# Half of the columns of the gathered tokens fetched as rows by indirect DMA, and turned late in a pass

## The chip, the cores and the metric

The kernel runs on one core of one Trainium2 chip. The metric is the device time of one execution in microseconds (us). TensorE is called PE, VectorE DVE, ScalarE ACT, GpSimd POOL and SyncE SP; PEld is PE's weight load, which overlaps its matmuls. SP only issues DMAs here.

## What is computed

One layer of a diffusion trunk runs on 384 tokens (128 context tokens and 256 latent ones) of 1024 columns in float32: a norm, four token mixers side by side, a merge, an output projection, then a mixture of experts, and a last norm. The change touches the experts alone:

```python
def block(args):
    rows, e = args
    xb = x_pad[rows]                                   # the tokens of this block, one per row
    return (jax.nn.silu(xb @ w1[e]) * (xb @ w3[e])) @ w2[e]

out = lax.map(block, (row_token, block_expert))        # every expert's tokens, block by block
return segment_sum(out * row_gate[:, None], row_token)[:T]   # each token's 8 experts added up, times their gates
```

There are 64 experts, of which each token takes 8. `w1` and `w3` of an expert are 1024x256, `w2` is 256x1024, so an expert has 3 MB of weights, and all of them are read once or more from memory.

## The kernel before

The token mixers and the router take the first 860 us or so. The routed experts follow, in `experts` (line 2643), in **passes**. A pass handles two **halves** `a_` of 128 places each, and a place is one token for one expert. The places of a half belong to two experts (`u`), in quarters of 32 places: one expert has three quarters and the other one, or each has two. A pass so reads the weights of four experts, 12.6 MB (12 DMAs of 1024 KB).

Everything is done with matrix products on PE:

- `sel` (line 2975, DVE) is a 0/1 matrix, tokens by 256 places, for both halves of the next pass. `gather` (line 2727) multiplies the normed tokens with it, so that `xg` holds the tokens of the 256 places with columns on the partitions, as the products of the experts want them. The tokens stand in two parts, `h2[HI]` and `h2[LO]` (`h_high` and `h_low` in rows), each of three tiles of 128 tokens. So one 128-column block of `xg` takes 6 products of 128x256; a job `G` makes two blocks in one bank, and the four jobs `G` of a pass make all eight.
- `H` (line 2826): the first two weight matrices on `xg`. ACT and DVE make `hid` from it. `HT` (line 2840) turns `hid`.
- `Y` (line 2863): the third matrix, in two jobs of 512 columns. ACT reads each bank into `y[HI]`, and then DVE subtracts that from the bank into `y[LO]` (line 3002), so that a bank of `Y` is free only when both are through.
- `S` (`turn`, line 2746) turns `sel` and the gates for the scatter. ACT reads the gates with four pairs of small instructions (line 2913) and then copies `selT` (line 2917). The copy into `selT` of half 0 also waits for `s_scat`, the end of the scatter that reads the old one.
- `scatter` (line 2735) adds `y` of the other half to the sums of the tokens, in banks 0 to 5, with 12 products in two groups of 6.

**Two banks for all jobs.** Six of PE's eight banks hold the sums. All other products of a pass are **jobs** that take banks 6 and 7 in turn, by their place in the list `JOBS`. `open_bank` lets PE wait until the job two places earlier in the list has been read by its last reader (`readers`: ACT, or DVE after it). ACT and DVE take their jobs in the order of the list too. This list is what sets the order of the work around the change. In the list before, `G` jobs are read by ACT and DVE in turn.

The order on PE in a pass is: half 0: H, scatter (first 6), HT, S of half 1, scatter (last 6), Y, Y; half 1: H, scatter, HT, four G, S of half 0, scatter, Y, Y. A first pass (written out, with the jobs of the router's plan, X and B, in it) and a last one (half 0 alone) stand around a loop. The first gather is made ahead of the first pass by four jobs `G0`.

SP refills the weights: `w13` of a half when its H is done, `w2` when its Y is done (line 3143 and 3147). PE waits for `w2` before the last two blocks of H, and for `w13` of the other half at the end of Y. POOL does nothing in this part until the very end (line 3132).

Of the kernel before, what the change touches and what calls it, by code (L numbers as in the profile page):

```python
# [14 lines left out]
P = 128  # L15
D = 1024
KD = D // P
NT = 3
T = NT * P
# [25 lines left out]
F32 = mybir.dt.float32  # L45
# [149 lines left out]
def trunk(nc, a, o):  # L195

    ctx = ExitStack()
    with ctx:
# [2185 lines left out]
        def _(pool):  # L2384
# [139 lines left out]
            for h in (1, 2, 3):  # L2524
                combine_last("merge", 3, h)
                if h < 3:
                    combine("merge", 3, h + 1)
                add_branch(3, 2 * h, 2 * h + 2)
            expert_work["gpsimd"](pool)


# [72 lines left out]

def expert_tiles(ctx, nc):


    def sb(name, *shape, dt=F32):  # L2610
        return name, ctx.enter_context(nc.sbuf_tensor(name, list(shape), dt))

    return dict([
        sb("xg", P, KD, 2 * P),
        sb("hid", P, FE),
        sb("sil", P, FE),
        sb("hidT", P, 2, P),
        sb("gslot", P, 2),
        sb("gate_parts", P, 2, NT, 2),
        sb("flags", P, 8),  # L2620
        sb("where", P, 16),
        sb("got", P, 4),
        sb("pad", P, 206),
        sb("w13", P, 2, 2, 2, KD, FE),
        sb("w2", P, 2, 2, 2, D),
        sb("sel", P, NT, 8, QUARTER, dt=F32R),
        sb("selT", P, 2, T, dt=F32R),
        sb("y", P, 2, D, dt=F32R),
        sb("quarter_places", P, NT, 8 + NX),
        sb("quarter_gates", P, NT, 8 + NX),  # L2630
        sb("expert_of", P, 2, NX // 4, dt=mybir.dt.int32),
        sb("rounds", P, 2, dt=mybir.dt.int32),
        sb("rowsE", P, 2, T),
        sb("farther", P, T),
        sb("steps", P, 2, 32),
        sb("plan", P, 4, NX),
        sb("turn_by", P, NT, TURN, dt=F32R),
        sb("g2row", P, 2, D),
        sb("final_gain", P, D),
    ])  # L2640


def experts(ctx, nc, a, o, psum, x, h2, mod_parts, ident_r, ident, ss, sq, sums, places, gates, iota, tiles, s_w13, s_rowsT, s_out):


    def sem(name):
        return ctx.enter_context(nc.semaphore(name))
# [10 lines left out]
    gated = spare[:, NT * D:2 * NT * D].rearrange("p (t n) -> p t n", t=NT)  # L2658


    s_filled = sem("job_filled")
    s_read = {"act": sem("act_took"), "dve": sem("dve_took")}
    s_w2 = [sem(f"down_{a_}_landed") for a_ in range(2)]
# [14 lines left out]


    AHEAD = [("G0", 0, j) for j in range(4)] + [("B", 0, 0), ("B", 0, 1), ("X", 0, 0), ("S0", 0, 0)]  # L2680
    GATHERS = [("G", 0, j) for j in range(4)]
    JOBS = [("H", 0, 0), ("HT", 0, 0), ("S", 1, 0), ("Y", 0, 0), ("Y", 0, 1), ("H", 1, 0), ("HT", 1, 0)] + GATHERS + \
           [("S", 0, 0), ("Y", 1, 0), ("Y", 1, 1)]
    JOBS_LAST = [("H", 0, 0), ("HT", 0, 0), ("Y", 0, 0), ("Y", 0, 1)]
    JOBS_FIRST = AHEAD + [("H", 0, 0), ("X", 0, 1)] + JOBS[1:5] + \
                 [("X", 0, 2), ("B", 0, 2), ("X", 0, 3), ("B", 0, 3), ("X", 0, 4)] + JOBS[5:]
# [1 line left out]

    def readers(job):
        kind, _, i = job  # L2690
        return {"H": ("act", "dve"), "HT": ("act",), "S": ("act",), "S0": ("act",), "Y": ("act", "dve"), "X": ("dve",), "B": ("act",),
                "G": (("act",), ("dve",))[i % 2], "G0": (("act",), ("dve",))[i % 2]}[kind]

    READS = {(kind, by): [j for j in LISTS[kind] if by in readers(j)] for kind in LISTS for by in ("act", "dve")}
# [25 lines left out]
    def tensor_part(pe):  # L2720
        mm = nc.tensor.matmul

        def gather(j, out):
            for i in range(2):
                k = 2 * j + i
                for n, (part, t) in enumerate([(part, t) for part in (HI, LO) for t in range(NT)]):
                    last = mm(out[:, i * 256:i * 256 + 256], lhsT=h2[part][:, t, k * P:(k + 1) * P],  # L2727
                              rhs=sel[:, t, :, :], start=n == 0, stop=n == 2 * NT - 1)
            last.then_inc(s_filled, 1)

        def scatter(a_, lo, hi):

# [52 lines left out]
        def body(q, kind, quarters):  # L2785
# [13 lines left out]
            def close_bank(ins):  # L2799
                ins.then_inc(s_filled, 1)  # L2800
# [14 lines left out]
            for a_ in range(1 if last else 2):  # L2815
                H, HT = ("H", a_, 0), ("HT", a_, 0)
                ps = open_bank(H)
                if first and a_ == 0:
                    for by, i in (("act", 2), ("dve", 3)):
                        pe.wait_ge(s_read[by], read(q, by, ("G0", 0, i), kind))  # L2820
                    pe.wait_ge(s_w13[0], 64)
                for k in range(KD):
                    if k == KD - 2:
                        pe.wait_ge(s_w2[a_], 32 * q + 32)
                    for lo, hi, u in quarters:
                        ins = mm(ps[lo:hi, :], lhsT=xg[:, k, a_ * P + lo:a_ * P + hi],  # L2826
                                 rhs=w13[:, a_, u, :, k, :], start=k == 0, stop=k == KD - 1)
                close_bank(ins)

                add = not (first and a_ == 0)  # L2830
                if add:
                    pe.wait_ge(s_read["dve"], read(q, "dve", ("Y", 0, 1), kind) if a_ else read(q - 1, "dve", ("Y", 1, 1)))
                    scatter(1 - a_, 0, 6)
                else:
                    close_bank(plan_step(1, open_bank(("X", 0, 1))))

                ps = open_bank(HT)
                pe.wait_ge(s_read["dve"], read(q, "dve", H, kind))
                for f in range(2):
                    ins = nc.tensor.transpose(ps[:, f * P:(f + 1) * P],  # L2840
                                              hid[:, :].rearrange("s (p f) -> s f p", f=2)[:, f, :], ident[:, :])
                close_bank(ins)

                if a_ == 0 and not last:
                    close_bank(turn(1, open_bank(("S", 1, 0))))
                elif a_:
                    pe.wait_ge(s_sel, q + 2)
                    for job in GATHERS:
                        gather(job[2], open_bank(job))
                    pe.wait_ge(s_gq, q + 2)  # L2850
                    close_bank(turn(0, open_bank(("S", 0, 0))))
                if add:
                    scatter(1 - a_, 6, 12)

                for h in range(2):
                    ps = open_bank(("Y", a_, h))
                    if h == 0:
                        pe.wait_ge(s_read["act"], read(q, "act", HT, kind))
                    for f in range(2):
                        if (h, f) == (1, 1) and not last:  # L2860
                            pe.wait_ge(s_w13[1 - a_], 64 * q + 64 * (1 + a_))
                        for lo, hi, u in quarters:
                            ins = mm(ps[lo:hi, :], lhsT=hidT[:, f, lo:hi], rhs=w2[:, a_, u, f, h * W:(h + 1) * W],  # L2863
                                     start=f == 0, stop=f == 1)
                    close_bank(ins)
                if first and a_ == 0:
                    for i in (2, 3, 4):
                        close_bank(plan_step(i, open_bank(("X", 0, i))))
                        if i < 4:
                            close_bank(gate_row(i, open_bank(("B", 0, i))))  # L2870

        HALVES = [(0, 64, 0), (64, 128, 1)]
        THREE_AND_ONE = [(0, 32, 0), (32, 64, 0), (64, 96, 0), (96, 128, 1)]
# [88 lines left out]
    def vector_part(dve):  # L2962
# [22 lines left out]
        def take(q, job, kind):  # L2985
            what, a_, i = job
            dve.wait_ge(s_filled, filled(q, job, kind))
            if "act" in readers(job):
                dve.wait_ge(s_read["act"], read(q, "act", job, kind))
            ps = bank_of(job, kind)  # L2990
            if what == "H":
                dve.wait_ge(s_gslot, 8 * q + 4 + 4 * a_)
                ins = stt(hid[:, :], ps[:, FE:], gslot[:, a_:a_ + 1], sil[:, :], ALU.mult, ALU.mult)  # L2993
            elif what in ("G", "G0"):
                ins = v.tensor_copy(xg[:, 2 * i:2 * i + 2, :].rearrange("p k n -> p (k n)"), ps)
            elif what == "X" and i < 2:
                ins = v.tensor_copy(got[0:NE, :], ps[0:NE, 0:4])
            elif what == "X":
                ins = table(ps, i - 2)
            else:  # L3000
                hh = slice(i * W, (i + 1) * W)
                ins = tt(y[:, LO, hh], ps, y[:, HI, hh].bitcast(F32), ALU.subtract)  # L3002
            ins.then_inc(s_read["dve"], 1)
# [79 lines left out]
        select_gates(slice(0, 8), 1)  # L3083
        dve.wait_ge(s_copied, 2)
        flag_counts()

        def body(q, kind):
            first, last = kind == "first", kind == "last"
# [39 lines left out]

    def gpsimd_part(pool):
        for t in range(NT):  # L3130
            pool.wait_ge(s_gated, t + 1)
            nc.gpsimd.tensor_tensor(x[:, t, 0:W], x[:, t, 0:W], gated[:, t, 0:W], ALU.add).then_inc(s_added, 1)  # L3132


    def sync_part(sp):
# [17 lines left out]
        for u in range(2):  # L3153
            down(1, u, 2 + u)
        sp.dma_start(fg_row[:, :], a["final_g"].rearrange("(a n) -> a n", a=1).to_broadcast([P, D])).then_inc(s_fg, 16)
        sp.wait_ge(s_read["dve"], read(0, "dve", ("X", 0, 4), "first"))

        def refill(q, a_, at, kind):
# [76 lines left out]
```

## Time and profile before

| | |
|---|---|
| median of 3 runs | 1456.57 us (1455.64 to 1459.07) |
| the profiled execution | 1455.05 us, of which the span from first to last instruction is 1453.2 us |
| granted TensorE clock, mean | 0.992 |
| PE busy | 1414.5 us, 97% of the span |
| DVE, ACT, POOL busy | 554.2, 430.1 and 273.1 us |
| DMA | 310.52 MB |

The profile is that of one execution. A timeline row merges neighbouring instructions of one line; since matmuls overlap one another, the time from one row's start to the next one's start says what a group costs on PE, not its own length. "<-" in a row's idle note names what it waited for. In rows, a product of plain float32 counts as two instructions, one of the rounded type `fp32r` as one; `w` stands for `w13` and `w2`, `arena` and `late` are shared memory, and `late` holds the constants `iota` too.

### The profile page before, as it was taken

How to read it: one execution, taken by the hardware profiler on the slowest of the kernel's cores; microseconds unless marked ns; L12 is line 12 of the kernel's file. 1: busy time of each engine (PE TensorE's matmuls, PEld its weight loads, DVE VectorE, ACT ScalarE, POOL GpSimd, SP SyncE). 2: the span in 40 equal slices, each digit the busy share in tenths (PEclk: the TensorE clock that was granted, in tenths of full speed). 3: DMA queues.
4: the chain of work that ended last, by engine and by line, in shares of the span. 5: the costliest groups of instructions: out<-in, count | busy, mean ns of one | idle time of the engine just before them, and what ended most of it. 6: DMA issues, size and time to landing. Idle time of an engine off the chain costs nothing.

```text
span 1453.2 us, 21489 instructions
## 1 busy us (share of the span) xinstructions
PE 1414.5 (97%) x8214; PEld 1014.5 (70%) x8214; DVE 554.2 (38%) x1116; ACT 430.1 (30%) x1020; POOL 273.1 (19%) x212
## 2 busy tenths in 40 slices
PE   6999999999999989999999999999999999999996
PEld 2795898989988986889987865555455555555552
DVE  3477243875255576434221373111111121111114
ACT  3232221322544362223320322223222232222223
POOL 0440324314054642553141000000000000000001
PEclk9999999999999999999999999999999999999998
DMA  9440422214202439321136343999999999999981
GB/s 377 166 131 27 133 70 105 88 59 145 75 16 85 160 131 361 104 87 59 59 102 196 119 186 151 419 421 402 373 363 378 359 373 378 379 379 378 376 333 44
DMA packets 104386, 310.52 MB, mean 214 GB/s; under 512 B 9216, under 2 KB 69376, under 8 KB 75776
## 3 DMA queue, kind: packets, MB, share of 16 engines
q1 hardware_dynamic: 97984, 306.46, 55.3%
q10 hardware_dynamic: 6336, 3.15, 0.8%
q8 instruction: 45, 0.74, 0.2%
q14 instruction: 21, 0.17, 0.0%
HBM read 306.44 MB, written 3.15 MB: 213 GB/s over the span
## 4 chain that ended last, share of the span: by engine, by line
PE 93%; DVE 2%; DMA 2%; ACT 1%; POOL 0%; issue 0%; SPq 0%; POOLq 0%; DVEq 0%
PE banks L595 20%; PE banks L627 19%; PE banks L2826 16%; PE banks L2863 8%; PE banks L2735 7%; PE banks L2727 7%; PE banks L1016 4%; DMA ring<-in_ada_w 2%; PE banks L602 2%; PE banks L1162 1%; PE banks L853 1%; PE banks L678 1%; PE banks L746 1%; PE banks L1210 1%; PE banks L2746 1%; PE banks L741 1%
## 5 line engine op out<-in xcount | busy, mean ns | idle before, releaser
L2826 PE MATMUL banks<-w,xg 128*64 128x512 f32 (+1 forms) x1312 | 234.0, 595 | 0.0
L2826 PEld LDWEIGHTS banks<-w,xg 128*64 128x64 f32 (+1 forms) x1312 | 73.5, 127 | 154.0 <-issue 134.9
L627 PE MATMUL banks<-hT,ring 128*128 128x192 f32 x792 | 137.8, 327 | 0.8 <-DVE late L1764 0.8
L627 PEld LDWEIGHTS banks<-hT,ring 128*128 128x128 f32 x792 | 129.6, 190 | 3.2 <-DVE late L1764 1.1
L3132 POOL TENSOR_TENSOR x<-x,w 128x512 f32<-128x512 f32 x3 | 4.2, 1429 | 655.7 <-DVE w L3111 655.7
L2863 PE MATMUL banks<-w,hidT 128*64 128x512 f32 (+1 forms) x656 | 120.7, 597 | 0.3 <-ACT hidT L2903 0.3
L2735 PE MATMUL banks<-y,selT 128*128 128x512 f32 x384 | 104.3, 407 | 0.0
L627 PE MATMUL banks<-x,combos 128*128 128x192 f32 x528 | 97.4, 328 | 2.6 <-ACT late L1320 2.6
L627 PE MATMUL banks<-x,ring 128*128 128x192 f32 x528 | 97.0, 327 | 0.9 <-ACT late L1327 0.9
L3002 DVE TENSOR_TENSOR y<-banks,y 128x512 fp32r<-128x512 f32 x66 | 45.6, 691 | 133.1 <-ACT y L2919 133.1
L2735 PEld LDWEIGHTS banks<-y,selT 128*128 128x128 f32 x384 | 67.3, 189 | 37.6 <-issue 26.2
L2993 DVE SCALAR_TENSOR_TENSOR hid<-banks,gslot,sil 128x256 f32<-128x256 f32 x33 | 16.0, 484 | 200.0 <-ACT sil L2901 200.0
L627 PEld LDWEIGHTS banks<-x,combos 128*128 128x128 f32 x528 | 88.1, 191 | 2.8 <-issue 2.8
L627 PEld LDWEIGHTS banks<-x,ring 128*128 128x128 f32 x528 | 86.9, 190 | 1.4 <-ACT late L1327 1.2
L595 PE MATMUL banks<-yT,ring 128*128 128x384 f32 x256 | 85.7, 487 | 0.0
L595 PE MATMUL banks<-ring,hT 128*128 128x256 f32 x384 | 85.5, 385 | 0.0
L2863 PEld LDWEIGHTS banks<-w,hidT 128*64 128x64 f32 (+1 forms) x656 | 34.0, 126 | 69.2 <-issue 68.0
L595 PEld LDWEIGHTS banks<-ring,hT 128*128 128x128 f32 x384 | 73.9, 193 | 10.1
L1016 PEld LDWEIGHTS banks<-arena 128*128 128x128 f32 x568 | 67.6, 192 | 11.5 <-issue 7.8
L2901 ACT ACTIVATE sil<-banks 128x256 f32<-128x256 f32 x33 | 12.7, 383 | 209.2 <-PE banks L2826 209.2
L1016 PE MATMUL banks<-arena 128*128 128x128 f32 x568 | 72.5, 279 | 0.8 <-DVE arena L2284 0.4
L2727 PE MATMUL banks<-sel,h_high 128*128 128x256 f32 x408 | 71.6, 284 | 0.0
(461 smaller groups left out, 2090.2 us busy)
## 6 DMA issues: line engine op xcount, KB each, us to landing
w<-in_exp_w SPq DMA_DIRECT2D x198, 1024.0 KB, 8.9
ring<-in_w_in SPq DMA_DIRECT2D x46, 1024.0 KB, 5.1
ring<-in_ada_w SPq DMA_DIRECT2D x24, 1024.0 KB, 7.8
ring<-in_w_branch SPq DMA_DIRECT2D x8, 1024.0 KB, 6.1
ring<-in_w_out SPq DMA_DIRECT2D x4, 1024.0 KB, 6.5
arena<-in_sh_w SPq DMA_DIRECT2D x3, 1024.0 KB, 7.9
x<-in_x_sample SPq DMA_DIRECT2D x4, 512.0 KB, 8.5
arena<-in_t_last_layer SPq DMA_DIRECT2D x1, 1024.0 KB, 8.3
```

The lines of the kernel that those rows point to most:

```text
L595: last = mm(out, lhsT=lhsT, rhs=rhs, start=i == 0, stop=i == len(pairs) - 1)
L602: last = nc.tensor.transpose(ps[0:n, i * P:(i + 1) * P], src, ident[:, :])
L627: last = mm(out, lhsT=w[:, k, :], rhs=tokens[:, k, :], start=start and k == 0, stop=k == KD // 2 - 1, skip_group_check=not start)
L678: last = mm(ps[g * 32:(g + 1) * 32, :], lhsT=cond[:, k, :], rhs=w[:, g * W:(g + 1) * W], start=k == 0, stop=k == KD - 1)
L741: banks.close(mm(ps, lhsT=fnet[:, (2, 1)[ri], tok[t]], start=True, stop=True, rhs=fw3[:, order * W:(order + 1) * W]))
L1016: last = mm(ps[:, h * P:(h + 1) * P], lhsT=lhsT, rhs=rhs, start=True, stop=True)
L2727: last = mm(out[:, i * 256:i * 256 + 256], lhsT=h2[part][:, t, k * P:(k + 1) * P], rhs=sel[:, t, :, :], start=n == 0, stop=n == 2 * NT - 1)
L2735: ins = mm(psum[:, t * 2 + h, :], lhsT=selT[:, a_, t * P:(t + 1) * P], rhs=y[:, part, h * W:(h + 1) * W], start=False, stop=False)
L2826: ins = mm(ps[lo:hi, :], lhsT=xg[:, k, a_ * P + lo:a_ * P + hi], rhs=w13[:, a_, u, :, k, :], start=k == 0, stop=k == KD - 1)
L2863: ins = mm(ps[lo:hi, :], lhsT=hidT[:, f, lo:hi], rhs=w2[:, a_, u, f, h * W:(h + 1) * W], start=f == 0, stop=f == 1)
L2993: ins = stt(hid[:, :], ps[:, FE:], gslot[:, a_:a_ + 1], sil[:, :], ALU.mult, ALU.mult)
L3002: ins = tt(y[:, LO, hh], ps, y[:, HI, hh].bitcast(F32), ALU.subtract)
```

## The change

Half of the columns (`FROM_ROWS` = 512 of 1024) now come into `xg` another way. Ahead of the loop, POOL adds the two parts of columns 512 to 1023 of all tokens into `whole_rows`, and SP stores these 384 rows of 2 KB in a tensor in memory (`token_rows`). In each pass, PE finds the token number of each place with two new jobs `I` behind the Y jobs of half 0 (3 products with 2 columns each); DVE turns them into integers `row_of_place`; POOL issues two indirect DMAs, one per half, that fetch 128 rows of 2 KB each into `fetched`. Only the first two `G` jobs stay products. The other two, which keep their names in the list, now turn `fetched` with 8 transposes, and stand behind `S` of half 0 and the scatter, just ahead of the Y jobs of half 1.

```diff
@@ gpsimd, end of the mixers' part
+            for t in range(NT):
+                banks.emptied(pool, ("h2", t, 1))
+            pool.wait_ge(s_out.sem, 96)
             expert_work["gpsimd"](pool)
@@ expert_tiles
+        sb("token_ids", P, NT, 2, dt=F32R),
+        sb("row_of_place", P, 2, dt=mybir.dt.int32),
+        sb("fetched", P, 2, D - FROM_ROWS),
+        sb("whole_rows", P, NT, D - FROM_ROWS),
@@ experts
-    GATHERS = [("G", 0, j) for j in range(4)]
-    JOBS = [("H", 0, 0), ("HT", 0, 0), ("S", 1, 0), ("Y", 0, 0), ("Y", 0, 1), ("H", 1, 0), ("HT", 1, 0)] + GATHERS + \
-           [("S", 0, 0), ("Y", 1, 0), ("Y", 1, 1)]
+    GATHERS = [("G", 0, j) for j in range(2)]
+    TURNS = [("G", 0, j) for j in range(2, 4)]
+    JOBS = [("H", 0, 0), ("HT", 0, 0), ("S", 1, 0), ("Y", 0, 0), ("Y", 0, 1), ("I", 0, 0), ("I", 1, 0), ("H", 1, 0),
+            ("HT", 1, 0)] + GATHERS + \
+           [("S", 0, 0)] + TURNS + [("Y", 1, 0), ("Y", 1, 1)]
@@ tensor_part
+        def turn_rows(j, out):
+            for i in range(2):
+                at = (2 * j + i) * P - FROM_ROWS
+                for a_ in range(2):
+                    last = nc.tensor.transpose(out[:, (2 * i + a_) * P:(2 * i + a_ + 1) * P], fetched[:, a_, at:at + P], ident[:, :])
+            last.then_inc(s_filled, 1)
+
+        def rows_of_places(a_, out):
+            for t in range(NT):
+                ins = mm(out[:, 0:2], lhsT=pair_selection(a_, t), rhs=token_ids[:, t, :], start=t == 0, stop=t == NT - 1)
+            return ins
@@ body of a pass on PE, behind the scatter of a half
+                if a_ and not last:
+                    for job in TURNS:
+                        out = open_bank(job)
+                        if job[2] == 2:
+                            pe.wait_ge(s_fetched, 32 * q + 32)
+                        turn_rows(job[2], out)
@@ body of a pass on PE, behind Y of half 0
+                if a_ == 0 and not last:
+                    if first:
+                        pe.wait_ge(s_ids, 1)
+                    pe.wait_ge(s_sel, q + 2)
+                    for i in range(2):
+                        close_bank(rows_of_places(i, open_bank(("I", i, 0))))
@@ vector_part
+            elif what == "I":
+                ins = v.tensor_copy(row_of_place[:, a_:a_ + 1], ps[:, 0:1])
+        for t in range(NT):
+            ins = ts(token_ids[:, t, :], iota[:, 2 * P:2 * P + 1].to_broadcast([P, 2]), float(t * P), None, ALU.add)
+        ins.then_inc(s_ids, 1)
@@ gpsimd_part
+            nc.gpsimd.tensor_tensor(whole_rows[:, t, :], h2[HI][:, t, FROM_ROWS:].bitcast(F32), h2[LO][:, t, FROM_ROWS:].bitcast(F32),
+                                    ALU.add).then_inc(s_whole, 1)
+        pool.wait_ge(s_stored, 16 * NT)
+        def fetch(q, kind):
+            for a_ in range(2):
+                pool.wait_ge(s_read["dve"], read(q, "dve", ("I", a_, 0), kind))
+                ...
+                nc.gpsimd.indirect_dma_start(
+                    fetched[:, a_, :], None, rows[:, :],
+                    bass.IndirectOffsetOnAxis(ap=row_of_place[:, a_:a_ + 1], axis=0)).then_inc(s_fetched, 16)
+        fetch(0, "first")
+        n2 = count(pool, 1)
+        with pool.Fori(1, n2) as q:
+            fetch(q, "mid")
@@ sync_part, behind the load of the last norm's gains
+        for t in range(NT):
+            sp.wait_ge(s_whole, t + 1)
+            sp.dma_start(rows[t * P:(t + 1) * P, :], whole_rows[:, t, :]).then_inc(s_stored, 16)
```

The order of the instructions on PE changes at two places of each pass. The first is the step from Y of half 0 (`w,hidT`) to H of half 1 (`w,xg`), before:

```order
L2863 MATMUL banks<-w,hidT 32x512 [waits act_took]
L2863 MATMUL banks<-w,hidT 32x512 x3
L2861 ISA
L2863 MATMUL banks<-w,hidT 32x512 [waits gate_up_1_landed]
L2863 MATMUL banks<-w,hidT 32x512 x3
L2794 REGISTER_ALU
L2826 MATMUL banks<-w,xg 32x512 [waits dve_took]
```

and now, with the jobs `I` between them (`token_ids,sel`):

```order
L2898 MATMUL banks<-w,hidT 32x512 [waits gate_up_1_landed]
L2898 MATMUL banks<-w,hidT 32x512 x3
L2909 REGISTER_ALU
L2823 REGISTER_ALU [waits selection_ready]
L2757 MATMUL banks<-token_ids,sel 128x2 [waits dve_took]
L2757 MATMUL banks<-token_ids,sel 128x2 x2
L2823 REGISTER_ALU
L2757 MATMUL banks<-token_ids,sel 128x2 [waits dve_took]
L2757 MATMUL banks<-token_ids,sel 128x2 x2
L2823 REGISTER_ALU
L2855 MATMUL banks<-w,xg 32x512 [waits dve_took]
```

H of half 1 followed Y directly; now the six small products stand between, and the second group of three waits for `dve_took` once more than H did: the count stands for the read of the second Y bank there, and for the first one's in the group ahead. The second place is the step from S of half 0 (`turn_by,sel`) over the scatter (`y,selT`) to Y of half 1, before:

```order
L2746 MATMUL banks<-turn_by,sel 128x144 [waits act_took]
L2746 MATMUL banks<-turn_by,sel 128x144 x2
L2735 MATMUL banks<-y,selT 128x512 x6
L2794 REGISTER_ALU
L2863 MATMUL banks<-w,hidT 32x512 [waits act_took,dve_took]
L2863 MATMUL banks<-w,hidT 32x512 x7
L2794 REGISTER_ALU
L2863 MATMUL banks<-w,hidT 32x512 [waits act_took]
```

and now, with the turned rows (`ident,fetched`) between scatter and Y:

```order
L2775 MATMUL banks<-turn_by,sel 128x144 [waits act_took]
L2775 MATMUL banks<-turn_by,sel 128x144 x2
L2764 MATMUL banks<-y,selT 128x512 x6
L2823 REGISTER_ALU
L2752 MATMUL banks<-ident,fetched 128x128 [waits rows_fetched,dve_took]
L2752 MATMUL banks<-ident,fetched 128x128 x3
L2823 REGISTER_ALU
L2752 MATMUL banks<-ident,fetched 128x128 [waits act_took]
L2752 MATMUL banks<-ident,fetched 128x128 x3
L2823 REGISTER_ALU
L2898 MATMUL banks<-w,hidT 32x512 [waits act_took]
L2898 MATMUL banks<-w,hidT 32x512 x7
```

Two groups of four transposes stand there now. The second waits for ACT's read of S, and Y for ACT's read of the first group; before, Y's first job waited for a read of the last gather, which was long past.

## Rows read from the trace of the kernel before

**Rows 1.** Of the page, the busy times; then DMA in 40 slices.

```profile
PE 1414.5 (97%) x8214; PEld 1014.5 (70%) x8214; DVE 554.2 (38%) x1116; ACT 430.1 (30%) x1020; POOL 273.1 (19%) x212
...
DMA  9440422214202439321136343999999999999981
GB/s 377 166 131 27 133 70 105 88 59 145 75 16 85 160 131 361 104 87 59 59 102 196 119 186 151 419 421 402 373 363 378 359 373 378 379 379 378 376 333 44
```

**Rows 2.** The chain of waits in time order, 952 to 986: start us, us, what.

```profile
952.44 6.87 PE banks L2826 x64
...
966.42 6.87 PE banks L2826 x64
...
974.88 0.23 PE banks L2840 x2
975.11 5.61 PE banks L2727 x48
980.72 0.29 PE banks L2746 x3
981.01 1.43 PE banks L2735 x6
982.44 3.57 PE banks L2863 x32
986.01 4.27 PE banks L2826 x37
```

**Rows 3.** All gather products (line 2727): duration ns min/median/max, first and last start.

```profile
L2727 PE MATMUL banks<-sel,h_high x408: 277/280/684, 867.8 to 1417.0; 128*128 128x256 f32 x136
...
L2727 PE MATMUL banks<-sel,h_low x408: 277/278/283, 868.5 to 1417.3; 128*128 128x256 f32 x136
```

**Rows 4.** Timeline by engine around the end of Y of half 0: start us, us.

```profile
966.49 0.60 ACT L2919 ACTIVATE y<-banks 128x512 fp32r<-128x512 f32 x1 [1.12 <-PE banks L2863]
...
965.40 0.69 DVE L3002 TENSOR_TENSOR y<-banks,y 128x512 fp32r<-128x512 f32 x1 [2.55 <-ACT y L2919]
967.12 0.69 DVE L3002 TENSOR_TENSOR y<-banks,y 128x512 fp32r<-128x512 f32 x1 [1.02 <-ACT y L2919]
...
966.14 0.23 PEld L2826 LDWEIGHTS banks<-w,xg 128*32 128x32 f32 x8 [0.63 <-DVE y L3002]
...
966.24 2.75 PE L2826 MATMUL banks<-w,xg 128*32 128x512 f32 x23
```

**Rows 5.** The same around the scatter of half 1.

```profile
979.36 0.60 ACT L2905 ACTIVATE xg<-banks 128x512 f32<-128x512 f32 x1 [2.20 <-PE banks L2727]
...
982.44 0.20 ACT L2913 ACTIVATION_READ_ACCUMULATOR gate_parts<-banks 32x1 f32 x1
982.66 0.49 ACT L2917 ACTIVATE selT<-banks 128x384 fp32r<-128x384 f32 x1
...
982.37 3.64 PE L2863 MATMUL banks<-w,hidT 128*32 128x512 f32 x32
```

**Rows 6.** The first pass, DVE and PE.

```profile
899.96 0.96 DVE L2975 TENSOR_TENSOR sel<-late,quarter_places 128x768 fp32r<-128x768 f32 x1
...
901.04 0.18 DVE L2983 TENSOR_TENSOR turn_by<-quarter_gates,turn_by 128x24 fp32r<-128x24 f32 x1
...
898.90 3.65 PE L2826 MATMUL banks<-w,xg 128*64 128x512 f32 x16
```

**Rows 7.** Two stretches: span, busy by engine, clock, DMA share, GB/s.

```profile
952.16:985.73 33.57, 33.57 (x278) 17.09 (x274) 6.34 (x11) 8.95 (x28) 0.00 (x0) 1.00 1.01 421
...
1120.00:1154.00 34.00, 34.00 (x184) 17.99 (x182) 6.50 (x12) 8.94 (x28) 0.00 (x0) 1.00 0.93 375
```

**Rows 8.** Landing of the weights (line 3143), us from issue.

```profile
DMA to landing us min/median/max: 4.8/9.1/21.7
```

**Rows 9.** Of the page: POOL's addition of 512 columns.

```profile
L3132 POOL TENSOR_TENSOR x<-x,w 128x512 f32<-128x512 f32 x3 | 4.2, 1429 | 655.7 <-DVE w L3111 655.7
```

**Rows 10.** DVE's small read of a bank, ns.

```profile
L2997 DVE COPY got<-banks x2: 144/148/152, 876.2 to 886.7; 64x4 f32<-64x4 f32 x2
```

More of the change, by code:

```diff
@@ L2603, in _ @@
             expert_work["sync"](sp)
+FROM_ROWS = D // 2
 def expert_tiles(ctx, nc):
@@ L2658, in experts @@
     gated = spare[:, NT * D:2 * NT * D].rearrange("p (t n) -> p t n", t=NT)
+    token_ids, row_of_place, fetched, whole_rows = (tiles[n] for n in ("token_ids", "row_of_place", "fetched", "whole_rows"))
+    rows = nc.dram_tensor("token_rows", (T, D - FROM_ROWS), F32, kind="Internal").ap()
+    s_whole, s_stored, s_ids = sem("whole_rows_ready"), sem("token_rows_stored"), sem("token_ids_ready")
+    s_fetched, s_row = sem("rows_fetched"), sem("row_of_place_seen")
     s_filled = sem("job_filled")
@@ L2690, in readers @@
         kind, _, i = job
-        return {"H": ("act", "dve"), "HT": ("act",), "S": ("act",), "S0": ("act",), "Y": ("act", "dve"), "X": ("dve",), "B": ("act",),
+        return {"H": ("act", "dve"), "HT": ("act",), "S": ("act",), "S0": ("act",), "Y": ("act", "dve"), "X": ("dve",), "B": ("act",), "I": ("dve",),
                 "G": (("act",), ("dve",))[i % 2], "G0": (("act",), ("dve",))[i % 2]}[kind]
@@ L3130, in gpsimd_part @@
         for t in range(NT):
+            nc.gpsimd.tensor_tensor(whole_rows[:, t, :], h2[HI][:, t, FROM_ROWS:].bitcast(F32), h2[LO][:, t, FROM_ROWS:].bitcast(F32),
[4 more added lines that the diff above has]
+                pool.wait_ge(s_read["dve"], read(q, "dve", ("I", a_, 0), kind))
+                pool.wait_ge(s_read["dve"], read(q, "dve", ("I", a_, 0), kind))
+                pool.sem_inc(s_row, 1)
+                nc.gpsimd.indirect_dma_start(
[6 more added lines that the diff above has]
+        for t in range(NT):
             pool.wait_ge(s_gated, t + 1)
@@ L3155, in sync_part @@
         sp.dma_start(fg_row[:, :], a["final_g"].rearrange("(a n) -> a n", a=1).to_broadcast([P, D])).then_inc(s_fg, 16)
+        for t in range(NT):
+            sp.wait_ge(s_whole, t + 1)
+            sp.dma_start(rows[t * P:(t + 1) * P, :], whole_rows[:, t, :]).then_inc(s_stored, 16)
         sp.wait_ge(s_read["dve"], read(0, "dve", ("X", 0, 4), "first"))
```

## The prediction

> **What bounds the kernel now.** I read the page's busy times first: PE is busy for 97% of the span, no other engine for more than 38% [rows 1]. In the experts' part the DMA engines are nearly full too (slices 26 on: 9 tenths, 363 to 421 GB/s), so the next question is which of the two sets the pace. The chain of waits says PE: from one H of half 0 (952.44) to the next (986.01) it runs through PE's products alone, and a pass lasts 33.57 us [rows 2]. A pass moves 12.58 MB of weights. In the stretch 952 to 986 the DMA engines catch up on a backlog and reach 421 GB/s, at which those take 29.9 us; later they move only what PE asks for, 375 GB/s at a share of 0.93 [rows 7]. So DMA could follow a pass down to some 30 us, and PE's own sequence is what an edit must shorten. PE's clock is granted in full there (1.00, the 2.4 GHz level), in both stretches.
>
> **What the change removes.** Half the gather products of a pass. The 48 of line 2727 take 5.61 us of the chain [rows 2], 0.117 us each; 24 go, **-2.80 us a pass**. The trace has 816 of them [rows 3], so 17 gathers; one is made ahead and stays, so 16 passes change: the first, and 15 in the loop.
>
> **What it adds at the end of Y of half 0 (jobs I).** Six small products, and a hand-over. Before, H of half 1 took the bank of the first Y job: DVE ends its subtraction at 965.40 + 0.69 = 966.09, PE loads weights at 966.14 and multiplies at 966.24 [rows 4], so 0.15 us from the end of a read to the next product. PE lost next to nothing, because the second Y job ran meanwhile. Now that bank goes to the first job I, and the second I takes the bank of the *second* Y job. ACT reads that one from 966.49 on and DVE is done at 967.12 + 0.69 = 967.81 [rows 4]. PE has nothing to run in between but three small products: the first product of the second I starts at 967.96. Three products with these same `sel` weights and 144 columns take 0.29 us (S [rows 2]); I take that for three with 2 columns as well, since the weight load is the same. H starts at 968.25 instead of 966.24: **+2.01 us**. H also needs DVE's conversion of the first I, 0.15 us [rows 10] from 967.81 on, which with 0.15 us of hand-over allows 968.11, so it does not bind, and that is the lower bound as well: +1.87. The upper: the three at the gather's 0.117 us and one more 0.1 us for a load, +2.2. Nothing is earned back behind H, which PE is then in.
>
> **What it adds between scatter and Y of half 1 (turned rows).** Eight transposes; two of float32 take 0.23 us (974.88 [rows 2]), so four take 0.46. But again the banks decide. The first group takes the bank of the second G, which is long free, and runs at 982.44. The second takes the bank of S, which ACT gives back only after four gate reads (the last ends at 982.44 + 0.20 = 982.64) and the copy of `selT`, 982.66 + 0.49 = 983.15 [rows 5]. ACT then copies the first group into `xg`; the like took 0.60 us (979.36 [rows 5]), so to 983.77. Y's first job takes *that* bank: 983.77 + 0.15 = 983.92, instead of 982.37 [rows 5]: **+1.55 us**. The second group (983.30 to 983.76) fits inside, and DVE's read of it (0.69 us, to about 984.9 with its end and hand-over) is over before Y's second job wants the bank at 983.92 + 1.8. Bounds: the gate reads start 0.3 us behind S whatever else, so little can be gained, +1.4; if ACT's copy starts 0.15 us late, +1.7.
>
> **Sum of a pass in the loop:** -2.80 + 2.01 + 1.55 = **+0.76 us**, with +0.47 to +1.10 as ends. Times 15: +11.4 us.
>
> **The first pass.** There `sel` is made late: DVE ends it at 899.96 + 0.96 = 900.92, while H of half 1 started at 898.90 and the gathers needed `sel` only later [rows 6]. The jobs I need it in front of H: first product at 901.07, three in 0.29 us, the last one's own duration about 0.28 [rows 3] to 901.64; DVE is free from 901.22 [rows 6], converts in 0.15 us, and H starts at about 901.94: +3.0. With -2.80 and +1.55 this is +1.8 us (1.4 to 2.3).
>
> **What I cost at nothing.** POOL's three additions (1.43 us each [rows 9]) and the three stores behind them lie 40 us ahead of the first fetch on engines that wait; even behind weights, whose landings take at most 21.7 us [rows 8], they are in time. If they were not, only the first pass would wait. DVE's three tiny instructions for the token numbers fall into an idle gap, about 0.5 us if not. POOL's own queue holds nothing but fetches until the end. The last pass and the tail are the old ones.
>
> **The fetches** are the unknown: no row shows an indirect DMA. POOL can issue both about 0.4 us behind the start of H (968.6); the first turned row is wanted when the scatter ends, in the new time at 982.44 + 2.01 - 2.80 = 981.65. That leaves **13.0 us** for 0.52 MB. From below, nothing waits. From above, a weight DMA of 1 MB takes 9.1 us in the median and 21.7 at most [rows 8], behind its own kind in a queue, and 21.7 would be 8.7 us too late. The fetches are four times smaller and in another queue, so I take the median's side: in time. The bytes also go through the same DMA engines: 13.1 MB a pass at 421 GB/s is 31.1 us, still below a pass of 34.3, so the weights stay in time too.
>
> The Trainium skill (DMA: Bandwidth & Descriptors, "Queues, rings and completion order") says that each DMA engine goes round between the rows of queues that have work, packet by packet; by that rule a fetch does not stand behind the queued weights. Its fit for a DMA issued from GpSimd ("Anatomy of one DMA") gives an estimate of 2.0 us + 262144 B / 436e3 B per us = 2.6 us for each, well inside the 13.0. The same page ("Issuing engines are not separate DMA queues") speaks against the change in that DMAs of all engines share the 16 DMA engines and interleave; by the rows above that costs bandwidth that PE does not ask for. No row here shows either at work.
>
> **Total:** 11.4 + 1.8 = +13.2 us, ends +8.5 and +18.8. The profiled execution took 1455.05 us, span 1453.2; it becomes 1468.3. The median of the runs is 1.5 us above that execution, and I forecast for the median: 1456.57 + 13.2 = **1469.8 us**, 0.9% slower.
>
> **Rivals.**
> - *The hand-overs are hidden* and only the products count. For it: ACT and DVE are idle for two thirds of the time, so their reads could seem free. Against: each new wait stands in PE's order with only 0.3 to 0.5 us of work in front of it, and the reads behind it last 0.6 and 0.69 us in sequence [rows 4, 5]. Then a pass changes by -2.80 + 0.58 + 0.92 = -1.30 us, 16 passes by -21: 1436. Chance 0.06. With only the first hidden, -2.80 + 0.58 + 1.55 = -0.67, so 1446, chance 0.03; with only the second, +0.13, so 1459, chance 0.05, which is no change.
> - *The rows come late.* PE then waits at the first transpose in each pass for what the landing takes above 13.0 us. For it: the DMA engines are full when the fetches are issued, and the largest landing is 21.7 us [rows 7, 8]; against: size and queue. At 15 us it costs 2 more a pass: 1470 + 32 = 1502; at 21.7, 1470 + 139 = 1609. Chance 0.08.
> - *DMA becomes the bound*: it would need passes under 31.1 us, which only the first rival comes near (32.3). It changes no number.
>
> **How the numbers follow.** Forecast 0.78, hidden 0.06, half hidden 0.03 and 0.05, late rows 0.08. A measurement of this kernel tells changes of about 0.2%, some 3 us, from none. So faster 0.09; same 0.05 and a hundredth of the forecast's low end, 0.06; slower 0.85. The range takes the forecast's ends (1465 to 1475), some slack for a duration that no row has, and the near part of the late rows: 1461 to 1482.
>
> **What would show it.** In the profile after: gather products 24 a pass, 2.8 us; about 1.1 us without a PE product between the two groups of small products, ended by DVE's subtraction into `y` (L3045); about 0.7 us before Y of half 1, ended by ACT's copy into `xg` (L2946); no wait for the fetched rows; a pass of 34.3 us; the clock still 1.00. I am wrong if H of half 1 starts less than 0.8 us later behind Y, if a wait for the fetches stands at the transposes, or if the clock falls in the new gaps.

## The result, and the profile after

| | before | after |
|---|---|---|
| median of 6 runs each | 1456.46 us (1451.84 to 1459.15) | **1469.76 us** (1464.05 to 1471.42) |
| ratio, 95% interval | | 1.0091 (1.0072 to 1.011) |
| profiled execution, span | 1453.2 us | 1467.8 us |

The changed kernel is slower by 0.9%. Of the page after, the busy times and the chain by engine; then the chain by engine of the page before:

```profile
PE 1406.9 (96%) x8054; PEld 998.9 (68%) x8054; DVE 560.9 (38%) x1151; ACT 428.8 (29%) x1020; POOL 307.1 (21%) x247
...
PE 89%; ACT 4%; DVE 3%; DMA 2%; issue 1%; POOL 0%; POOLq 0%; SPq 0%; DVEq 0%
```

```profile
PE 93%; DVE 2%; DMA 2%; ACT 1%; POOL 0%; issue 0%; SPq 0%; POOLq 0%; DVEq 0%
```

PE is busy for 7.6 us less than in [rows 1], and the span is 14.6 us longer: on the chain PE's share falls from 93% to 89%, and ACT and DVE go from 1% and 2% to 4% and 3%. That is the removed work and the waits in its place.

A pass of the loop as in [rows 2], cut into its stretches on PE, each from the start of one group to the start of the next (medians of three or four passes between 1090 and 1250 us; e1 to e9 are the experiments below):

| kernel | Y of half 0, with I | H half 1 | G | turned rows | S | last scatter | pass |
|---|---|---|---|---|---|---|---|
| before | 3.48 | 6.97 | 5.69 | | 0.29 | 1.52 | 33.60 |
| after | 3.58 + 1.92 | 7.01 | 2.88 | 1.51 | 0.29 | 1.43 | 34.27 |
| e1 | 3.59 + 1.92 | 7.02 | 2.89 | 1.52 | 0.29 | 1.43 | 34.29 |
| e2 | 3.64 + 0.76 | 6.96 | 2.89 | 1.52 | 0.29 | 1.43 | 33.12 |
| e3 | 3.58 + 1.92 | 7.02 | 2.90 | 1.36 | 0.38 | 1.50 | 34.30 |
| e4 | 3.64 + 0.76 | 6.97 | 2.88 | 1.36 | 0.37 | 1.53 | 33.17 |
| e5 | 3.64 + 0.76 | 6.96 | 2.94 | 0.51 + 0.93 | 0.29 | 1.43 | 33.31 |
| e6 | 3.58 + 1.92 | 7.02 | 2.89 | 1.52 | 0.29 | 1.43 | 34.30 |
| e7 | 3.49 | 6.96 | 3.30 | | 0.39 | 1.53 | 31.30 |
| e8 | 3.58 + 1.92 | 7.01 | 5.69 | | 0.29 | 1.52 | 35.66 |
| e9 | 3.64 + 0.76 | 6.97 | 1.51 + 1.50 | 0.64 + 0.94 | 0.29 | 1.52 | 33.52 |

The stretches left out are the same in all to 0.2 us (HT of half 1 before the first turn is the largest, 0.36 in e5 against 0.15). The first turn of e5 lasts between 0.38 and 0.64 us from pass to pass. From after's chain of waits, the two new pieces; first the end of Y of half 0:

```profile
1002.30 3.62 PE banks L2898 x32
1005.94 0.61 ACT y L2960
1006.57 0.70 DVE y L3045
1007.32 0.49 PE banks L2757 x3
1007.81 2.26 PE banks L2855 x17
```

[rows 2] had H (6.87) directly behind Y. Now the chain leaves PE for ACT's copy of the second Y bank and DVE's subtraction and returns with the second group of three products (L2757). The second place, S (L2775) to Y (L2898):

```profile
948.11 2.80 PE banks L2744 x24
950.91 0.30 PE banks L2775 x3
...
952.85 0.50 ACT selT L2958
953.39 0.66 PE banks L2752 x4
954.05 3.57 PE banks L2898 x32
```

Behind S (0.30) the chain is on ACT, from the gate reads left out here to the copy of `selT`, back on PE for the second group of transposes (L2752), then Y. The scatter, which was on the chain in [rows 2], has dropped out of it: it is shorter than ACT's reads, but only just. The copy of `selT` must wait for its end too, and in the timeline of the pass shown next the last product of the scatter ends at 1019.55 + 1.60 = 1021.15 and the last gate read at 1021.35, so faster gate reads alone would win 0.2 us at most. The two places in the timeline of one pass, the one of the first chain above, and the waits of PE there, added up between 860 and 1466 us (us, times, the longest):

```profile
1007.32 0.49 PE L2757 MATMUL banks<-token_ids,sel 128*128 128x2 f32 x3 [1.02 <-DVE y L3045]
...
1021.37 0.49 ACT L2958 ACTIVATE selT<-banks 128x384 fp32r<-128x384 f32 x1
1021.76 0.59 ACT L2946 ACTIVATE xg<-banks 128x512 f32<-128x512 f32 x1
...
1021.91 0.66 PE L2752 MATMUL banks<-ident,fetched 128*128 128x128 f32 x4 [0.33 <-ACT selT L2958]
...
1022.50 3.64 PE L2898 MATMUL banks<-w,hidT 128*32 128x512 f32 x32
```

```profile
PE banks L2757 <- DVE y L3045: 12.1, 12, 1.0
PE banks L2752 <- ACT selT L2958: 5.2, 16, 0.3
PE banks L2757 <- DVE row_of_place L3038: 3.0, 3, 1.0
```

The third row is the same wait as the first, in three more passes: there the view names DVE's next instruction, which starts 0.08 us before the subtraction ends.

In these rows the idle time in front of a matmul is what the overlap of matmuls leaves to be seen; the table above has the whole cost.

### The profile page after: what moved, and what is told of

The parts are those of the page before. It is cut to its first block, busy times and chain, and to the rows that moved or that the text cites. A ratio compares the mean times of both kernels' runs of the same rounds, so it can differ in the third digit from the quotient of the medians.

```text
span 1467.8 us, 21418 instructions
## 1 busy us (share of the span) xinstructions
PE 1406.9 (96%) x8054; PEld 998.9 (68%) x8054; DVE 560.9 (38%) x1151; ACT 428.8 (29%) x1020; POOL 307.1 (21%) x247
## 4 chain that ended last, share of the span: by engine, by line
PE 89%; ACT 4%; DVE 3%; DMA 2%; issue 1%; POOL 0%; POOLq 0%; SPq 0%; DVEq 0%
PE banks L595 20%; PE banks L627 19%; PE banks L2855 16%; PE banks L2898 8%; PE banks L2764 5%; PE banks L1016 5%; PE banks L2744 3%; DMA ring<-in_ada_w 2%; PE banks L1162 1%; PE banks L853 1%; ACT gate_parts L2954 1%; PE banks L602 1%; PE banks L678 1%; PE banks L746 1%; DMA ring<-in_w_in 1%
## 5 line engine op out<-in xcount | busy, mean ns | idle before, releaser
L3186 POOL DMA_INDIRECT fetched<-token_rows,row_of_place x32 | 30.4, 951 | 529.7 <-DVE row_of_place L3038 524.8
L2898 PE MATMUL banks<-w,hidT 128*64 128x512 f32 (+1 forms) x656 | 120.7, 597 | 0.3 <-ACT hidT L2944 0.3
L2898 PEld LDWEIGHTS banks<-w,hidT 128*64 128x64 f32 (+1 forms) x656 | 34.0, 126 | 66.4 <-issue 62.4
L2419 POOL TENSOR_TENSOR ring<-ring,combos 128x512 f32<-128x512 f32 x33 | 45.2, 1369 | 129.4 <-PE banks L627 129.2
```

What stands on the lines that cost most here:

```text
L2419: s_combos.on(g.tensor_tensor(a11, a12, combos[:, 1], ALU.subtract))
L3186: nc.gpsimd.indirect_dma_start(fetched[:, a_, :], None, rows[:, :], bass.IndirectOffsetOnAxis(ap=row_of_place[:, a_:a_ + 1], axis=0)).then ...
```

## Experiments

**e1, the first pass as before.** The first pass keeps its four gather jobs by products; it has no I, no fetch and no turned rows (shortened here):

```diff
     JOBS_FIRST = AHEAD + [("H", 0, 0), ("X", 0, 1), ...
-                 ... JOBS[5:]          # I, I, H, HT, G, G, S, turned, turned, Y, Y
+                 ... ("H", 1, 0), ("HT", 1, 0)] + GATHERS + TURNS + [("S", 0, 0), ("Y", 1, 0), ("Y", 1, 1)]   # all four by products
```

> The changed kernel, but the first pass gathers all eight blocks by products as before (no jobs I, no fetch, no turned rows in it); the 15 passes of the loop are untouched. My account says that the first pass cost 2.8 us over before (44.24 against 41.47 us from H to H), of which the wait for the selection matrix ahead of the jobs I is 2 us and the halved clock behind that gap another 2 us, against 2.8 us of products saved. So the first pass returns to 41.5 us, a pass in the loop stays at 34.27 us, and the time falls from 1469.8 to about 1467. Rival: the slow clock in the first pass has nothing to do with the gap (before shows a slow H there too); then the first pass still has an H of 9.3 us and the time stays at 1469 to 1470.

Measured: 1466.49 us, ratio to before 1.0073 (1.0048 to 1.0098). First pass 41.62 us, a pass of the loop 34.29. As expected; the first pass is taken up again with the clock, at the end.

**e2, the token numbers inside Y.** On e1: both I jobs become one, put between the two halves of the first Y job, in columns 432 to 435 of the bank that S of half 1 used; S is read by then:

```diff
+                        if (a_, h, f) == (0, 0, 1) and not last and not first:
+                            pe.wait_ge(s_sel, q + 2)
+                            pe.wait_ge(s_read["act"], read(q, "act", ("S", 1, 0), kind))
+                            at = NT * TURN
+                            for i in range(2):
+                                ins = rows_of_places(i, bank_of(("I", 0, 0), kind)[:, at + 2 * i:at + 2 * i + 2])
+                            close_bank(ins)
```

> e1 with both jobs I made one, put between the two halves of the first Y job of half 0, where the bank of S is free, so that no product waits for DVE's read of the second Y bank. Hand-over theory: from the start of Y to the start of H of half 1 it takes 3.46 us (before) plus 0.6 us for six small products, 4.05, instead of 5.51; a pass goes from 34.27 to 32.8 us, 15 passes give -22 us against e1: 1445. The fetches start about 4 us earlier. Rival (the time of a pass is set by the DMA engines once PE is faster, because the fetches share them): 13.1 MB at the 375 to 385 GB/s seen late in the loop would hold a pass at 34 us, and the time at 1467.

Measured: 1445.34 us, ratio 0.9934 (0.991 to 0.9957), so faster than before and 21 us under e1. Its chain at this place:

```profile
1025.84 0.99 PE banks L2910 x8
1026.83 0.76 PE banks L2759 x6
1027.59 2.71 PE banks L2910 x24
1030.30 6.87 PE banks L2860 x64
```

Y, products, Y, H, with no other engine between them. The six products cost 0.76 us there, and the piece is 1.1 us shorter than after's. The pass fell to 33.12 instead of the 32.8 expected because the products and the broken Y take 0.92 us over a plain Y where I had taken 0.6. No product of PE waits for a DMA.

**e3, the turns ahead of S.** On e1, and only the order changes:

```diff
-           [("S", 0, 0)] + TURNS + [("Y", 1, 0), ("Y", 1, 1)]
+           TURNS + [("S", 0, 0)] + [("Y", 1, 0), ("Y", 1, 1)]
```

> e1 with the turned rows moved ahead of S of half 0, directly behind the two gather jobs, so that scatter covers ACT's reads as before. Hand-over theory: the stretch from the start of the scatter to the start of Y of half 1 returns from 2.95 to 1.52 us, and eight transposes cost 0.92 us: -0.5 us a pass, 33.76 us, -8 us against e1: 1459. Rival: the rows are wanted 1.7 us earlier and now come late: the second fetch is issued 1.65 us behind the start of H of half 1 and its landing took 6.8 to 9.0 us, so it is there 8.4 to 10.7 us behind that start, and the first transpose would run at 11.4; under the theory it is in time by 0.7 us or more, under the rival PE waits there and the pass stays above 34 us.

Measured: 1465.20 us, ratio 1.0057 (1.0039 to 1.0076); against e1's 1466.49 no difference that these runs can tell. The pass is 34.30 us. Neither theory was right. No wait for the rows shows up; instead the chain reads

```profile
1048.72 2.81 PE banks L2745 x24
...
1051.56 0.70 DVE xg L3036
...
1052.30 0.66 PE banks L2753 x4
1052.96 0.29 PE banks L2776 x3
1053.25 1.42 PE banks L2765 x6
1054.67 1.41 PE banks L2898 x9
```

Between the gathers (L2745) and the second turn (L2753) stands DVE's read of the last gather bank, 0.70 us. The first group of transposes runs beside it and is shorter. So the wait for S went and a wait for the gather came: 1.36 + 0.38 + 1.50 = 3.24 us from the end of the gathers to Y, where after has 0.29 + 1.43 + 1.51 = 3.23. A short job in a chain of two banks exposes the read of whatever stands ahead of it.

**e4, both moves.** e2 and e3 in one.

> e1 with both moves (e2 and e3). If the two hand-overs are all that ate the gain, and are independent: a pass is 33.59 - 2.80 + 0.6 + 0.92 = 32.3 us, and the time 1467 - 15 x 1.97 = 1437.5, faster than before by 1.3%. Rival: DMA becomes the bound; at 421 GB/s its floor is 31.1 us a pass, so if it reaches less than 405 GB/s the pass ends between 32.3 and 34 us, and PE shows waits for weights.

Measured: 1450.19 us, ratio 0.9959 (0.9945 to 0.9973), a pass of 33.17 us. The two moves do add up as seen one by one (-1.17 and 0), but e3's part is nothing. PE waited for no weights. That this median is 4.9 us above e2's is mostly the granted clock of the runs: at a mean of 0.991, e2 took 1449.33 us and e4 1449.98 to 1450.72.

**e5, one turn ahead of the gathers.** On e2:

```diff
-           GATHERS + [("S", 0, 0)] + TURNS + [("Y", 1, 0), ("Y", 1, 1)]
+           TURNS[0:1] + GATHERS + [("S", 0, 0)] + TURNS[1:2] + [("Y", 1, 0), ("Y", 1, 1)]
```

> e2 with the first group of turned rows directly behind HT of half 1 and ahead of the two gather jobs; the second stays behind the scatter. In e3 the turns stood behind each other there and the second waited for DVE's read of the last gather, so the 1.5 us stayed 1.4. Two-bank theory: each turn now has a job of over a microsecond on its other side, and only two rests of a wait are left: the two turns cost 1.0 us instead of 1.51, a pass 32.6 us against e2's 33.12, the time about 1438. Rival (rows late): the first turn wants both fetches 8.7 us behind the start of H of half 1; issued as in e2 they have landed about 7.3 us behind it, by their longest landing of 9.9 us seen only just; if late, PE waits at the transposes and the pass is 33 us or more.

Measured: 1452.78 us, ratio 0.9973 (0.9956 to 0.999); a pass of 33.31 us, longer than e2's. My expectation missed that with one turn less behind the scatter it is Y's first job that takes the bank of S. Its waits on PE:

```profile
PE banks L2910 <- ACT selT L2968: 5.0, 15, 0.3
PE banks L2754 <- DMA fetched<-token_rows,row_of_place: 1.1, 3, 0.7
```

Y (L2910) waits for `selT`, and the rows come at the last moment: three passes wait for them, 0.7 us at most. The first turn has a short neighbour too: the gather behind it takes the bank of HT, and in ten of the fifteen passes its weights load 0.05 us after ACT's read of that bank. e9 shows the same.

**e6, no fetch in the loop.** PE waits only once for rows, those of the first pass:

```diff
         with pool.Fori(1, n2) as q:
-            fetch(q, "mid")
+            for a_ in range(2):
+                pool.wait_ge(s_read["dve"], read(q, "dve", ("I", a_, 0), "mid"))
+                pool.sem_inc(s_row, 1)
```

> The changed kernel with the indirect DMAs left out of the loop (the first pass fetches once, and the loop turns the same rows again; POOL and PE keep all other instructions), so the experts get wrong tokens in half of their columns. If the fetches cost nothing (my account): a pass stays at 34.27 us and the time at 1469.8. Rival (contention of 0.52 MB a pass, or POOL's work disturbing DVE): the pass falls by up to 1.2 us, the time by up to 18.

Measured: 1468.50 us, ratio 1.0079 (1.0057 to 1.0101), a pass of 34.30 us. With or without the fetches the pass is the same to 0.03 us: they cost nothing in this kernel.

**e7, the removal alone.**

```diff
-                        gather(job[2], open_bank(job))
+                        gather(job[2], open_bank(job), 1)      # one block of two
```

> The kernel before with half of the gather products of each pass left out and nothing in their place: each gather job makes one block of its two, its bank is read whole as before, so half of the columns of the tokens hold old numbers. All jobs, banks and waits stay. This is what the removal alone is worth: 24 products at 0.117 us, -2.8 us a pass, 16 passes: -45 us, about 1410; a pass of 30.8 us. Rival: DMA holds the pass at 33 us or so (375 GB/s seen late in the loop), or ACT's and DVE's reads of banks now filled every 0.7 us do: then clearly less than 2.8 us a pass goes.

Measured: 1418.30 us, ratio 0.9749 (0.9723 to 0.9775), a pass of 31.30 us, which is 2.3 us less and not 2.8. The gathers take 3.30 us on PE for half the products:

```profile
1060.93 3.20 PE banks L2727 x24
1064.13 0.40 PE banks L2746 x3
```

24 products at 0.117 us would be 2.80. The four banks are now filled in 0.7 us each, while ACT reads one in 0.60 and DVE in 0.69 us, plus hand-over [rows 4, 5]. In this pass the third job's weights load at 1062.32, and ACT's read of the first bank ended at 1061.67 + 0.60. DMA gave 12.58 MB in 31.30 us, 402 GB/s; no product of PE waits for it, and two weight loads do, for 1.1 us together. So even this upper bound of what could be won is partly held by the two banks.

**e8, the jobs I alone**, all gathers kept, no fetch, no turns (in the loop):

```diff
-    GATHERS = [("G", 0, j) for j in range(2)]
-    TURNS = [("G", 0, j) for j in range(2, 4)]
+    GATHERS = [("G", 0, j) for j in range(4)]
+    TURNS = []
```

> The kernel before (all eight blocks gathered by products) plus the jobs I of the loop at their place behind Y of half 0, and nothing else of the change that runs in the loop: no fetch, no turned rows. It prices the first hand-over by itself: from Y's start to H's start of half 1 5.5 us instead of 3.5, +2.0 us a pass, 15 passes: +30 us, about 1486. Rival (products alone count): +0.6 us a pass, +9 us, about 1465.

Measured: 1484.41 us, ratio 1.0205 (1.018 to 1.023), a pass of 35.66 us, +2.06. The first hand-over is worth 2 us a pass by itself, and six products of two columns made the kernel 2% slower.

**e9, turns by half between the gathers.** On e2. Not shown below: each half has a semaphore of its own, and the two gathers change readers, so that DVE reads the first one:

```diff
-            ("HT", 1, 0)] + GATHERS + [("S", 0, 0)] + TURNS + [("Y", 1, 0), ("Y", 1, 1)]
+            ("HT", 1, 0)] + [job for pair in zip(TURNS, GATHERS) for job in pair] + [("S", 0, 0), ("Y", 1, 0), ("Y", 1, 1)]
...
+        def turn_rows(a_, out):
+            for i in range(4):
+                last = nc.tensor.transpose(out[:, i * P:(i + 1) * P], fetched[:, a_, i * P:(i + 1) * P], ident[:, :])
```

> e2 with each turn taking the rows of one half (four blocks of one half, so that the first waits for the first fetch alone, on a semaphore of its own) and the order HT, turn, gather, turn, gather, S, scatter, Y, Y. Two-bank theory: only the second gather still waits, 0.2 to 0.3 us for DVE's read of the first one, since a turn of 0.46 us is shorter than a read; nothing stands in front of Y any more. The turns then cost 1.2 us instead of 1.51, a pass goes from 33.12 to 32.8 us, the time to about 1440.5. Rival (rows late): in e5 the first turn waited up to 0.7 us in some passes for the second fetch; if the first fetch is no earlier, the gain is eaten there and the pass stays at 33.1 us.

Measured: 1452.39 us, ratio 0.9982 (0.9972 to 0.9991), a pass of 33.52 us instead of the 32.8 expected. The rows are in time. The one wait expected is there (L2747 behind L3046):

```profile
1044.36 0.44 PE banks L2753 x4
...
1044.84 1.70 PE banks L2747 x12
...
1046.56 0.70 DVE xg L3046
...
1047.31 1.67 PE banks L2747 x12
1048.97 0.29 PE banks L2776 x3
```

but it is longer than expected: the second turn takes 0.94 us where I had counted 0.46 and 0.2 to 0.3. And there is a second wait that I had not expected, in front of the first gather. That one takes the bank of HT, and the turn ahead of it is too short to cover ACT's read of it:

```profile
1044.08 0.47 PEld L2753 LDWEIGHTS banks<-ident,fetched 128*128 128x128 f32 x4
1044.40 0.38 ACT L2950 ACTIVATE hidT<-banks 128x256 f32<-128x256 f32 x1 [1.39 <-PE banks L2873]
...
1044.83 0.42 PEld L2747 LDWEIGHTS banks<-sel,h_high 128*128 128x128 f32 x3 [0.28 <-ACT hidT L2950]
```

ACT is through at 1044.78, and the gather's weights load 0.05 us later, as in all fifteen passes. So the 0.64 us of the first turn is a wait for a bank as well, and e9 lost for the same reason as the change itself. The two gathers also take 3.01 us instead of 2.89; what those 0.12 us are stays open.

**e10, e2 once more**, beside e9:

> The kernel of e2 again, beside e9 on the same chip, so that the two can be compared: 33.12 us a pass and 1445 us by its first run.

Measured: 1447.75 us, ratio 0.9951 (0.9935 to 0.9966), 33.12 us a pass again. This version is 0.5 to 0.7% faster than the kernel before, in two series of runs.

## Why the prediction was right

The mechanism was right: the two hand-overs cost more than the removed products. The time (1469.8 forecast, 1469.76 measured) is closer than the working deserves, and that much is luck. The loop came out 1.2 us under its term and the first pass 1.0 us over, and the medians also hold a difference of clock: after's run at a mean clock of 0.993 took 1464.05 us and its run at 0.990 1468.83, against medians of 1453.19 and 1458.70 for before's runs at the same two values, so some 10 to 11 us at equal clock, where the medians differ by 13.3. The terms, against the table:

- *Gathers removed.* -2.80 a pass forecast, 5.69 to 2.88 measured, -2.81.
- *The hand-over at Y of half 0.* +2.01 forecast; 3.48 to 3.58 + 1.92 measured, +2.02. e8 adds it alone (+2.06 a pass), e2 takes it away (-1.17, what is left are the products themselves). This is shown.
- *The hand-over at the turned rows.* +1.55 forecast; 1.52 to 1.43 + 1.51 measured, +1.42. ACT began to copy the first group at 1021.76, 0.10 us before its copy of `selT` had ended (1021.37 + 0.49 = 1021.86), where I had put it behind the end. The sign that I had given, 0.7 us before Y ended by ACT's copy into `xg`, is not there as such: 0.33 us of PE's idle time stand before the second group, ended by `selT`, and only the weight load of Y waits for `xg`, 0.17 us. That the bank is the cause is shown less directly than for the first: e3 took the wait for S away and a wait for the gather bank of the same size appeared.
- *A pass in the loop.* +0.76 forecast, +0.67 measured. From the second pass's H to the last pass's H it is 504.06 us before and 514.21 after, so +10.2 us where +11.4 was forecast.
- *The first pass.* +1.8 forecast (2.3 at most), 41.47 to 44.24 measured, +2.8. The wait for `sel` is there; what I had not seen is that the clock plays a part in both numbers (below). Kernels whose first pass is the old one and ran at full clock took 39.97 us (e2, e4); after's 44.24 less the 2.2 us by which its H of half 1 was slow leaves 42.0, so the edit itself cost 2.1 us.
- *In time at no cost.* Fetches (e6), prologue stores, weights: right. The landing of a fetch, which no row had shown:

```profile
L3186 POOL DMA_INDIRECT fetched<-token_rows,row_of_place x32: 941/945/1155, 903.2 to 1420.8; - x32
...
DMA to landing us min/median/max: 6.8/7.8/9.0
```

The second one is issued 1.25 us behind the first, and both are there 8.8 to 10.4 us after the first issue, of the 12.85 us that PE left them (1008.14 to 1020.99). The median's side was the right one. The estimate of 2.6 us by the Trainium skill's fit (DMA: Bandwidth & Descriptors, "Anatomy of one DMA") does not hold beside this stream of weights; the landing took 7.8 us. e5 left the rows 10.2 us (1134.50 to 1144.73) and found the edge.

The rival of hidden hand-overs fell with e8 for the first one and, for the second, with the table and the chain (+1.42 us a pass); that of late rows with e6.

The rest of the span's +14.6: 1.7 us were lost before the first H (877.20 to 878.91), in code that is the same in both. Ahead of it the granted clock of after stood at 0.50 for 13.6 us in all, that of before for 10.2 us; one such stretch of each (columns as in the last section, the clock third from the end):

```profile
367.80:378.00 10.20, 10.20 (x37) 9.03 (x37) 4.19 (x15) 10.06 (x13) 0.00 (x0) 0.50 0.16 57
```

```profile
371.70:375.10 3.40, 3.40 (x9) 2.65 (x9) 0.26 (x2) 3.38 (x3) 0.00 (x0) 0.50 0.00 0
```

The other executions fit: the first H starts at 872.01 and 872.31 where the clock did not fall before it (e4, e8), and at 880.71 where it stood at 0.50 for 17.0 us (e6). So this part goes with the clock, not with the change.

## What to carry to other kernels

When all jobs of the bounding engine go through two banks in turn, a job is not priced by its own length. The job behind it can start only when the last reader of the job ahead of it is through, and a short job covers little of that time. Splitting or adding short jobs can so cost more than the long products they replace; ask of each new job whose bank it takes, when that one's *last* reader is through, and what the engine has to do meanwhile. Put a short job inside a long one, where its bank is already free (e2), rather than behind it, and expect that a moved job exposes another read (e3, e5, e9).

## What the runs showed of the hardware

**The clock falls once or twice in the first pass, in some executions.** Rows of after: stretch, span, busy by engine, granted clock, DMA share, GB/s:

```profile
893.00:899.20 6.20, 6.19 (x39) 4.79 (x37) 2.09 (x7) 1.19 (x2) 0.00 (x0) 1.00 0.00 0
899.20:902.60 3.40, 1.37 (x8) 1.38 (x8) 2.23 (x8) 0.00 (x0) 0.00 (x0) 0.65 0.03 5
902.60:905.00 2.40, 2.40 (x7) 0.74 (x8) 0.16 (x1) 0.00 (x0) 1.50 (x2) 0.50 0.90 307
905.00:908.00 3.00, 3.00 (x12) 0.99 (x10) 0.00 (x0) 0.00 (x0) 0.60 (x1) 0.65 1.01 425
908.00:912.00 4.00, 4.00 (x21) 1.18 (x16) 0.00 (x0) 0.07 (x1) 0.00 (x0) 1.00 1.00 395
```

PE had a gap of 2.0 us and then six short products (899.2 to 902.6), the clock was at 0.65 of full speed in that stretch and at 0.50, the 1.2 GHz level, in the first 2.4 us of H and part of the 3 us behind them (0.65); H took 9.30 us instead of 7.09. But it is not the gap alone: e10, without such a gap, and e2, the same kernel in another execution, at their two H of the first pass:

```profile
877.56:880.00 2.44, 2.44 (x9) 0.83 (x10) 0.96 (x7) 1.85 (x9) 0.00 (x0) 0.58 0.99 406
...
900.40:904.00 3.60, 3.60 (x11) 1.10 (x12) 2.07 (x7) 0.00 (x0) 0.00 (x0) 0.50 0.16 20
```

```profile
875.99:883.00 7.01, 7.01 (x33) 2.21 (x32) 0.96 (x7) 1.85 (x9) 0.00 (x0) 1.00 0.69 275
...
896.20:903.20 7.00, 7.00 (x33) 2.21 (x32) 2.07 (x7) 0.00 (x0) 0.00 (x0) 1.00 0.50 166
```

e10 was slow in both (8.78 and 9.45 us) and its first pass took 44.99 us, e2 in neither (7.09 both) and took 39.97. Before has it once, in its first H (8.58). These 5 us are more than a third of the 13 us that the change cost, so a comparison of first passes by one profile each misleads. The scatter between whole runs goes with the clock too: of before's 47 runs beside the experiments, the 21 with a mean granted clock of 0.993 or more have a median of 1453.15 us and none above 1455.17, the 20 with 0.991 or less a median of 1457.30 and none under 1454.97. What decides where it falls stays open, and so does whether the gap in after's first pass makes it fall more often (at H of half 1 it fell in both executions with that gap, after and e6, and in four of the ten without). In the loop the clock was 1.00 everywhere, gaps of about a microsecond in each pass included.

**A group of four float32 transposes took 0.38 to 0.39 us where nothing held what follows**, less than the 0.46 of two pairs. That is so in five passes of e5, in which the turn began late and the bank of HT was free when it was done; the weight loads of one of them follow each other without a gap:

```profile
1044.98 0.42 PEld L2754 LDWEIGHTS banks<-ident,fetched 128*128 128x128 f32 x4 [0.36 <-issue]
1045.37 0.42 PEld L2746 LDWEIGHTS banks<-sel,h_high 128*128 128x128 f32 x3
```

Of the longer times in the table, those that stand for one group (0.64, 0.93 and 0.94 us) end with a wait for a bank.
